# Gathering and turning the experts' rows by quarters: VectorE's 32x32 blocks in place of TensorE's turns

## The reference, cut to what matters

```python
aff = softmax(xf @ w_router)                  # per group: 1024 tokens x 16 experts
gate, idx = lax.top_k(aff.T, cap)             # cap = 128 tokens per expert
xe = xf[idx]                                  # 16 x 128 x 1024
hid = silu(xe @ w_gate) * (xe @ w_up)
ye = (hid @ w_down) * gate
y = zeros.at[idx].add(ye)                     # then x + gate2 * rmsnorm(y)
```

## Time and profile before

| | us |
|---|---|
| Timed runs, median of 3 | 2404.12 (2403.29 to 2409.57) |
| Span of the profiled execution | 2402.6 |
| Median less that span | 1.5 |
| PE busy in the span | 2296.1 (96%) |
| DVE busy | 1208.7 (50%) |
| ACT busy | 1103.8 (46%) |
| POOL busy | 603.2 (25%) |
| Expert stage, in the span | about 1266 to 2402.6 |

### The profile page before, as it was taken

The page is one execution under the profiler, slowest core; times in us unless marked ns, Lnnn a source line. Parts: engine busy times, 40 slices in busy tenths (PEclk is TensorE's granted clock), DMA queues, the critical chain, the costliest instruction groups (busy, mean ns, idle before and its releaser), DMA issues. The chain is left out here.

```text
span 2402.6 us, 35196 instructions
## 1 busy us (share of the span) xinstructions
PE 2296.1 (96%) x13583; PEld 1915.1 (80%) x13583; DVE 1208.7 (50%) x1881; ACT 1103.8 (46%) x1828; POOL 603.2 (25%) x676
## 2 busy tenths in 40 slices
PE   6999999999999999999947999999999999999997
PEld 4679989777899897667736888888888888888886
DVE  3222334554413346665566555544445556666655
ACT  4223444655433436665543444444444455555552
POOL 3004342443133324430021011111110122222434
PEclk9999999999999999999978999999999999999999
DMA  8835445658454459764547566666666678888785
GB/s 319 259 107 182 145 160 185 191 150 185 122 194 141 162 177 249 228 180 158 170 189 263 204 211 221 214 226 210 207 203 231 216 268 309 322 308 291 284 302 175
DMA packets 239040, 511.49 MB, mean 213 GB/s; under 512 B 36981, under 2 KB 128005, under 8 KB 235825
## 3 DMA queue, kind: packets, MB, share of 16 engines
q1 hardware_dynamic: 190960, 394.78, 49.0%
q0 software_dynamic: 47936, 114.77, 16.0%
HBM read 415.32 MB, written 93.69 MB: 212 GB/s over the span
## 5 line engine op out<-in xcount | busy, mean ns | idle before, releaser
L2492 DVE TENSOR_TENSOR moe_w_lo<-moe_wf,moe_w_hi 128x2048 fp32r<-128x2048 f32 x192 | 439.5, 2292 | 456.6 <-ACT moe_w_hi L2367 450.0
L2367 ACT ACTIVATE moe_w_hi<-moe_wf 128x2048 fp32r<-128x2048 f32 x192 | 367.8, 1916 | 551.4 <-PE moe_acc L2630 550.5
L2630 PE MATMUL moe_acc<-moe_w_hi,moe_x_hi 128*128 128x512 f32 x1024 | 401.7, 392 | 0.9 <-DVE moe_x_lo L2498 0.6
L2630 PE MATMUL moe_acc<-moe_w_hi,moe_x_lo 128*128 128x512 f32 x1024 | 398.9, 390 | 0.0
L2630 PE MATMUL moe_acc<-moe_w_lo,moe_x_hi 128*128 128x512 f32 x1024 | 398.4, 389 | 0.0
L2630 PEld LDWEIGHTS moe_acc<-moe_w_hi,moe_x_hi 128*128 128x128 f32 x1024 | 192.3, 188 | 40.7 <-DVE moe_x_lo L2498 0.8
L2630 PEld LDWEIGHTS moe_acc<-moe_w_hi,moe_x_lo 128*128 128x128 f32 x1024 | 192.2, 188 | 40.3
L2630 PEld LDWEIGHTS moe_acc<-moe_w_lo,moe_x_hi 128*128 128x128 f32 x1024 | 192.4, 188 | 38.9
L1793 PE MATMUL banks<-fr_w_hi,fr_h_hi 128*128 128x256 f32 x768 | 223.2, 291 | 0.0
L1793 PE MATMUL banks<-fr_w_lo,fr_h_hi 128*128 128x256 f32 x768 | 217.0, 283 | 0.0
L1793 PE MATMUL banks<-fr_w_hi,fr_h_lo 128*128 128x256 f32 x768 | 216.9, 282 | 0.0
(11 more groups left out here) (294 smaller groups left out, 4083.4 us busy)
## 6 DMA issues: line engine op xcount, KB each, us to landing
moe_wf<-in_w_expert_gate SPq DMA_DIRECT2D x64, 1024.0 KB, 4.9
moe_wf<-in_w_expert_up SPq DMA_DIRECT2D x64, 1024.0 KB, 4.9
moe_wf<-in_w_expert_down SPq DMA_DIRECT2D x64, 1024.0 KB, 5.8
fr_w_raw<-in_w_units SPq DMA_DIRECT2D x28, 1024.0 KB, 7.2
fr_bias<-in_na_bias SPq DMA_DIRECT2D x16, 1520.0 KB, 11.1
fr_a_w<-in_w_ada POOLq DMA_DIRECT2D x16, 1024.0 KB, 9.0
scratch_qk_t<-fr_stage SPq DMA_DIRECT2D x64, 256.0 KB, 2.5
scratch_vov<-fr_stage SPq DMA_DIRECT2D x96, 128.0 KB, 2.2
```

The costliest lines, as they stand in the source:

```text
L2367: nc.scalar.activation(w_hi[:, q, :, :], wf[:, q, :, :], ACT.Copy).then_inc(w_hi_ready, 1)
L2492: nc.vector.tensor_tensor(w_lo[:, q, :, :], wf[:, q, :, :], w_hi[:, q, :, :].bitcast(F32), ALU.subtract).then_inc(w_lo_ready, 1)
L2630: mm = nc.tensor.matmul(acc[:, j, b, :], x[:, g, k, :], w[:, q, a, h * HALF:(h + 1) * HALF], start=(k == 0 and i == 0), stop=(k == KC - 1 ...
```

## The change

The gather takes quarter rows. Partition 32q + n of `xe` receives, at position t, quarter q (256 columns) of the row of slot 32t + n. One indirect DMA now fetches 128 pieces of 1 KB, 4 of them per group, 8 per expert. Its row numbers, 4 x row + quarter, stand in `index_q`, made once. DVE then transposes 32x32 blocks, reading columns 2 apart. A whole group is one instruction, and it writes straight into the place that `x_lo` then takes over. ACT and DVE make `x_hi` and `x_lo` out of SBUF in one instruction per group. GATE and UP weights of experts 1 to 15 are loaded in the matching order of rows: 8 KB in one run per partition. Expert 0 keeps whole rows and PE's turn. SP's loop is written out; the other engines keep theirs. From expert 9 on, POOL issues the gather after the loads of each half of the final stage, one group per half, and no longer ahead of them.

```diff
+    by_chunk = [w.rearrange("e (q a p) n -> e q p a n", p=P, a=PIECE) for w in weights]
+    by_quarter = [w.rearrange("e (u q c a) n -> e q u c a n", u=4, q=NP, c=QT) for w in weights]
+    h2_quarters = io["h2"].rearrange("t (q n) -> (t q) n", q=4)
 ...
+        with nc.sbuf_tensor("moe_x_raw", [P, 2, GROUPS, KC, P], F32) as x_raw:
+            pass                                   # the place that x_lo takes
+            def gather(e, j, gs=range(GROUPS)):    # POOL
+                if isinstance(e, int) and e == 1:
+                    pool.wait_ge(first_turned, ONE + BK)
+                    pool.wait_ge(quarters_ready, 1)
+                else:
+                    pool.wait_ge(x_turned, ONE + (e - 1) * GROUPS)
 ...
+                for g in gs:
+                    for t in range(4):
+                        at = index_q[:, t, col(e, g)] if isinstance(e, int) else idx_in[:, j, t, g:g + 1]
+                        pool.indirect_dma_start(quarter_rows(g)[:, t, :], None, h2_quarters,
+                                                bass.IndirectOffsetOnAxis(ap=at, axis=0)).then_inc(gathered[g], 16)
             def body(e, j):                        # POOL
-                if not is_last(e, 2):
-                    gather(e + 2, j)
                 ns = window(e)
+                if not ns and not is_last(e, 2):
+                    gather(e + 2, j)
 ...
                         for n in half:
                             load_unit(n)
+                        if not is_last(e, 2):
+                            gather(e + 2, j, range(h, h + 1))
+            def x_out(e, j):                       # ACT
+                for g in range(GROUPS):
+                    act.wait_ge(x_turned, ONE + (e - 1) * GROUPS + g + 1)
+                    nc.scalar.activation(x_hi[:, j, g, :, :], x_raw[:, j, g, :, :], ACT.Copy).then_inc(x_hi_ready, 1)
+            each_slot = index_f[:, :].rearrange("r (t n) -> r t n", t=4).unsqueeze(2).to_broadcast([R, 4, 4, QT])
+            nc.vector.tensor_copy(index_rep[:, :, :, :], each_slot).then_inc(rep_ready, 1)   # DVE, ahead of index_c
 ...
+            def turn_x(e, j):                      # DVE, first in body(e - 1)
+                dve.wait_ge(piece_done, ONE + piece(e - 1, GATE, NP))
+                for g in range(GROUPS):
+                    dve.wait_ge(gathered[g], e * 64)
+                    columns = xe[:, g, :].rearrange("p (b c a) -> p b a c", c=QT, a=PIECE)
+                    turned = x_raw[:, j, g, :, :].rearrange("p m (t r) -> p t m r", t=4)
+                    nc.vector.transpose(turned, columns).then_inc(x_turned, 1)
                 else:                              # DVE body
+                    turn_x(e + 1, 1 - j)
                     split(e + 1, GATE, range(0, 2))
-                    turned_out(e + 1, x_hi[:, 1 - j], x_lo[:, 1 - j], 1 - j, x_hi_ready, x_ready)
+                    x_out(e + 1, 1 - j)
-                    products(e, UP, j, x_hi[:, j], x_lo[:, j], range(1, 2))     # PE body
-                    turn_x(e + 1, 1 - j)
-                    products(e, UP, j, x_hi[:, j], x_lo[:, j], second)
-                    pe.wait_ge(x_ready, ONE + e * BK + 2 * BK)
+                    products(e, UP, j, x_hi[:, j], x_lo[:, j], range(1, NP))
+                    pe.wait_ge(x_ready, ONE + (e + 1) * GROUPS)
+                    pe.wait_ge(ye_ready, ONE + e * GROUPS)
```

More of the change, by code:

```diff
@@ L2165, in experts @@
         gcol_ready = s.sem("gcol_ready")
-        gathered = s.soft_sem("gathered")
+        gathered = [s.soft_sem(f"gathered{g}") for g in range(GROUPS)]
+        first_turned, first_hi_ready, first_ready = (s.sem(f"first_{n}") for n in ("turned", "hi_ready", "ready"))
+        rep_ready, rep_turned, quarters_ready = (s.soft_sem(n) for n in ("rep_ready", "rep_turned", "quarters_ready"))
         x_turned = s.sem("x_turned")
@@ L2224, in load @@
                         sp.wait_ge(w_lo_ready, ONE + piece(e, step, q) - NP + 1)
-                    sp.dma_start(wf[:, q, :, :], mats[step][e, q]).then_inc(w_loaded[q], 16)
+                    rows = by_chunk[step] if e == 0 or step == DOWN else by_quarter[step]
+                    sp.dma_start(wf[:, q, :, :], rows[e, q]).then_inc(w_loaded[q], 16)
             load(0, GATE, True)
@@ L2240, in body @@
                 load(e, DOWN)
-            over_experts(sp, body)
+            for e in range(NE):
+                body(e, e % 2)
         @block.gpsimd
@@ L2248, in _ @@
             nc.gpsimd.memset(mhalf[:, :], -0.5)
+            for q in range(4):
+                pool.drain()
+                nc.gpsimd.memset(quarter[q * QT:(q + 1) * QT, :], float(q))
+            pool.drain()
             identity(nc, pool, ident)
@@ L2261, in _, with gather_first @@
             by_expert = lambda t, e: t[:, :].rearrange("p (g e) -> p g e", g=GROUPS)[:, :, bass.ds(e, 1)].squeeze(2)
[L2263 to L2268, removed]
-                    pool.drain()
[L2270 to L2274, removed]
+            def gather_first():
+                for g in range(GROUPS):
+                    at = bass.IndirectOffsetOnAxis(ap=index_c[:, col(0, g)], axis=0)
+                    pool.indirect_dma_start(xe[:, g, :], None, io["h2"], at).then_inc(first_x[g], 16)
+                    if g == 0:
+                        nc.gpsimd.memset(row0[:, :], 0.0).then_inc(first_begun, 1)
+            def gather(e, j, gs=range(GROUPS)):
[4 more added lines that the diff above has]
+                    pool.wait_ge(x_turned, ONE + (e - 1) * GROUPS)
+                if not isinstance(e, int) and 0 in gs:
+                    by_quarter = index_q[:, :, :].rearrange("p t (g e) -> p t g e", g=GROUPS)
+                    nc.gpsimd.tensor_copy(idx_in[:, j, :, :], by_quarter[:, :, :, bass.ds(e, 1)].squeeze(3))
+                    pool.drain()
+                for g in gs:
[3 more added lines that the diff above has]
+                                                bass.IndirectOffsetOnAxis(ap=at, axis=0)).then_inc(gathered[g], 16)
             def scatter(e, j):
@@ L2617, in _ @@
             nc.tensor.transpose(acc[:, 0, 0, 0:R], gate[:, :], ident[0:R, 0:R]).then_inc(top_turned, 1)
+            pe.wait_ge(rep_ready, 1)
+            for t in range(4):
+                mm = nc.tensor.transpose(acc[:, 1, 0, t * R:(t + 1) * R], index_rep[:, t, :, :].rearrange("r q n -> r (q n)"), ident[0:R, 0:R])
+            mm.then_inc(rep_turned, 1)
             pe.wait_ge(cols_ready, ONE + 2)
@@ L2635, in products, with turn_first, turn_h @@
                         mm.then_inc(half_done, 1)
-            def turn(rows, j, done, bs=range(BK)):
+            def turn_first(g):
+                pe.wait_ge(first_x[g], 16)
+                for b in range(2 * g, 2 * g + 2):
+                    for k in range(4):
+                        c = (b % 2) * 4 + k
+                        mm = nc.tensor.transpose(acc[:, 0, b, k * P:(k + 1) * P], xe[:, g, c * P:(c + 1) * P], ident[:, :])
+                    mm.then_inc(first_turned, 1)
+            def turn_h(e, j, bs=range(BK)):
+                pe.wait_ge(hid_ready, ONE + e * BK + bs[-1] + 1)
                 for b in bs:
```

59 lines of the change are left out of this document (34 added, 25 removed).

## The result

| | before | after |
|---|---|---|
| Timed runs, median, us | 2403.82 (2403.29 to 2409.57) | 3150.81 (3148.66 to 3159.74) |
| Span of the profiled execution, us | 2402.6 | 3146.9 |

The changed kernel is 31% slower: ratio 1.3111, interval 1.3088 to 1.3133. The forecast was 2379.0, range 2374 to 2391. Two executions fell in a slower state and are in no ratio: one of the kernel before (3866.98 us) and one of the version with the gather ahead (2713.96 us), whose median of 2405.36 would be 2404.98 without it.

The account below looks back on a forecast made before the run. PE, busy 96% of the span, was taken as the bound until near the end. 2402.6 - 26.2 (turns) + 0.3 (start) + 1.0 (end) = 2377.7 us span, 2379.2 with 1.5 around it; given as 2379.0, range 2374 to 2391.

Parts of the forecast that it names:

- DMA: Weight loads and gather traffic: GATE and UP's 8 KB runs unchanged at 2.5 us per MB, gather 1.5 us more per expert.
- 15 us in hand per load: GATE and UP loads in the expert stage: each was said to have some 15 us to spare.
- The sign named for this case: Profile after the change: GATE and UP loads landing later than DOWN's would show the forecast wrong; no size given.
- the gather's 1.5 us: DMA engines, per expert: extra time for the gather's megabyte in 1024 packets instead of 256, bounds 0 and 8.1 us.
- Rival 3: GATE and UP loads at half rate make DMA the bound in five experts: about 2434 us; chance 5%.
- PE: Expert stage: 15 turns of 1.75 us go, 26.2 us in all; expert period falls from 68.85 to 67.1 us.
- DVE: Two added transposes per expert, 1.23 us each, 2.5 us per pair, fit into DVE's idle time.
- The room of 10.4 us: DVE, per expert: the transpose pair may take 10.4 us before PE has to wait for `x_lo`.
- DVE becomes late: Transposes over 5.2 us each make PE wait for `x_lo` in 15 experts: about 2403 us at 6 us each; chance 4%.
- Gather: POOL's indirect DMAs, eight per expert instead of two: four cost 7 us, range 5 to 13.2.
- The tail: Kernel's end: expert 13's gathers delay its roots and scatter, leaving a loss of 1.0 us.
- Start: Path to the first gather: DVE's copy of 64x512 numbers with the drain adds 0.3 us, bounds 0 and 1.

## Why the prediction was wrong, by its own steps

**DMA: the failed step.** "I take no change" for the 8 KB runs of GATE and UP, between bounds of half and twice the time, so the sum has no term for the loads. Measured: 107 GB/s where 412 to 428 were had, four times the time per byte, outside these bounds. The 2.5 us per MB of the term became 9.8. I asked what the runs and addresses would do to a packet and never how many engines would share them. It could be seen in the diff: the new pattern has a dimension of 4 ahead of the partition's rows, and this 4 does not merge. With 15 us in hand per load, a number for which the prediction shows no working, a load of 1 MB that takes 9.8 us looks harmless by itself. The sum decides: 8 of them are 78.4 us, in a period of 67.1. The sign named for this case came: ACT waited 1069 us for GATE and UP and 12.9 for DOWN. A small slip stands beside it: with the gather's 1.5 us the busy expert comes to 59.3 us of DMA work and not to 61; it changes nothing.

**Rival 3** had the right kind of end, DMA as the bound and slower than before, but 2434 was far too little. It took half the rate where it was a quarter, and so charged only the five busy experts, while a quarter rate puts all 15 over their period. And its cause, the 1 MB between the quarters, is refuted: the groups close together are as slow (ratio 1.3126), and rows 32 KB apart on one stride lose nothing (0.9894). By the Trainium skill (DMA: Bandwidth & Descriptors, Latency and other measured facts) a large power of two between partitions can halve the rate. No run here shows it: within a group, neighbouring partitions of the weight loads stood 4 to 32 KB apart in all of them.

**PE: right.** 1.75 us per turn, period 67.05 to 67.08 in the run with the old loads, against 67.1. 26.2 us of its 30.5 us of span gain are these. Another 2.3 are chance: in that profile the last index step, at the end of code that the change doesn't touch, starts at 1274.72 in place of 1277.04, and over the fourteen profiled executions of all kernels it lies anywhere from 1273.27 to 1279.34.

**DVE: right.** 1.23 was forecast for a transpose and 1.22 measured. The room of 10.4 us was right to 0.1. What the rival "DVE becomes late" lacked is the clock: past the room a us of stall cost 61.1 / 38.2 = 1.6 us of time.

**Gather: right in price, short in effect.** Four DMAs were to cost 7 us; in the version with a single stride a set took 8.3, from 1996.57 to 2004.89, and its roots came at 2009.67, where PE was busy throughout. In expert 13, with the old loads, four took 6.4 us, and the roots followed at once. The tail was to lose 1.0; whole rows gained 2.3 in the whole kernel, less than the intervals tell apart. With the old loads no such loss is seen: from the scatter of expert 13 to the end it is 2372.1 - 2251.76 = 120.3 us, and 2402.6 - 2277.84 = 124.8 before, with one turn of 1.75 us in it. The step undervalued their placement: ahead of the loads, the same eight DMAs cost 26 to 29 us.

**Start.** 0.3 us was forecast. From the last index step to the first product it was 1283.39 - 1274.72 = 8.67 us with the old loads and 1285.32 - 1277.04 = 8.28 before: 0.4.

With the old loads the kernel ran at 2374.56, with one stride at 2376.56; the sum, which put the loads at nothing, said 2379.0. The other terms together came out within 4.4 us, some of it chance as said above. The one that failed cost 776 us (3150.81 - 2374.56), 27 times what the rest gained.

## What to carry to other kernels

Ask of every DMA first how many of the 16 engines will carry it: look at its slowest dimension on both sides after merging, and write layouts in which the partitions have one stride. In a profile, flat stretches far below the known rate at a low share of the engines (here a quarter of 428 GB/s at 0.2 to 0.3) and too few packets per load tell of it. Add up a load's new duration over a whole period; slack of a single load says nothing about the queue. And when many small indirect DMAs are added to an in-order queue, put them behind what others wait for.

## What the runs showed of the hardware that I had not expected

- Loads spread over 4 engines moved 104 to 108 GB/s in flat stretches, over 8 engines 116 to 135, over 16 up to 428. From 4 to 8 the rate is far from doubled: with 8 engines each moved some 16 GB/s, with 4 or 16 some 26.8. What held the 8 back stays open.
- DMAs of 32 partitions kept the engines busy 0.93 to 0.99 of the window for 214 to 220 GB/s, where those of 128 took 0.66 for 216. 16 groups of 8 partitions took 0.86 for 224. The cause of neither is settled; only the HBM addresses are excluded. In the calm window it cost PE nothing; in the whole kernel it cost 65 to 112 us against the same kernel with the old loads.
- A transpose of 128x1024 in 32x32 blocks took 1.22 us with source columns 2 apart and 2.15 with columns 8 apart.
- One indirect DMA, 0.94 us beside an idle DVE, took 7.29 beside splits and subtractions that followed each other without a gap.
- Behind a stall of 2.36 us on PE the granted clock read 0.68, 0.50 and 0.97 in three stretches of 2 us, and the stall cost 1.9 us on top of itself.
